# Both feed-forward sublayers as seven products of quarters, on one NeuronCore

## The reference, cut

```python
def swiglu(x, w_gu, w_down):
    a, u = jnp.split(x @ w_gu, 2, axis=-1)      # 1024 -> 2 x 2816
    return (jax.nn.silu(a) * u) @ w_down        # 2816 -> 1024

def ffn_sublayer(x, w_gu, w_down, g, b):
    return layer_norm(ALPHA * x + 0.5 * swiglu(x, w_gu, w_down), g, b)
```

## Time and profile before

| | us |
|---|---|
| runs (3): median, lowest, highest | 1947.2, 1946.07, 1953.2 |
| profiled execution: span from first to last instruction | 1943.7 |
| first feed-forward stretch | 27.86 to 427 |
| second feed-forward stretch | 1519.4 to 1921 |

### The profile page before, as it was taken

How to read it: one execution, slowest core, us unless ns; L and a number is a source line. 1 busy time by engine, 2 the same in 40 slices (tenths; PEclk the granted TensorE clock), 3 DMA queues, 4 the chain that set the end, 5 groups by cost and what they waited for, 6 DMA issues and landing times.

```text
span 1943.7 us, 33105 instructions
## 1 busy us (share of the span) xinstructions
PE 1804.9 (93%) x13247; PEld 1699.9 (87%) x13247; DVE 778.9 (40%) x1081; ACT 667.4 (34%) x899; POOL 85.2 (4%) x113
## 2 busy tenths in 40 slices
PE   6999999998997768999989999999999899999996
PEld 5999999987997537878768999869998799999996
DVE  2333332234223875756663223344345433333123
ACT  3333331124223555666563222124322433332111
POOL 0000000000002420000000000110000000000002
PEclk9999999999997998999989999999999999999998
DMA  4222222230440015767752232062223022222221
GB/s 142 91 90 91 89 84 82 81 108 22 133 133 23 1 51 176 273 228 249 242 169 91 87 98 84 17 215 66 91 91 100 22 86 87 89 90 84 92 97 46
DMA packets 146659, 203.75 MB, mean 105 GB/s; under 512 B 5538, under 2 KB 127330, under 8 KB 146594
## 3 DMA queue, kind: packets, MB, share of 16 engines
q1 hardware_dynamic: 145442, 198.35, 31.4%
q0 software_dynamic: 1152, 4.46, 0.6%
HBM read 191.39 MB, written 11.40 MB: 104 GB/s over the span
## 4 chain that ended last, share of the span: by engine, by line
PE 88%; DVE 4%; ACT 4%; issue 2%; DMA 0%; SPq 0%; POOL 0%; ACTq 0%; POOLq 0%; DVEq 0%
PE ps L297 68%; PE ps L1201 4%; PE ps L1232 3%; PE ps L1187 2%; PE ps L974 1%; PE ps L988 1%; PE ps L614 1%; PE ps L1624 1%; PE ps L1211 1%; PE ps L1616 1%; PE ps L1248 1%; PE ps L699 1%; PE ps L1198 1%; ACT aT L1069 1%; PE ps L981 0%
## 5 line engine op out<-in xcount | busy, mean ns | idle before, releaser
L297 PE MATMUL ps<-xh,w_hi_t 128*128 128x272 f32 x2432 | 510.1, 291 | 25.3 <-DVE xl L651 18.3
L297 PE MATMUL ps<-xh,w_lo_t 128*128 128x272 f32 x2432 | 505.9, 290 | 0.0
L297 PE MATMUL ps<-xl,w_hi_t 128*128 128x272 f32 x2432 | 504.2, 289 | 0.0
L283 DVE TENSOR_TENSOR w_lo_t<-w_raw,w_hi_t 128x2048 fp32r<-128x2048 f32 (+1 forms) x112 | 252.4, 2254 | 519.2 <-ACT w_hi_t L279 519.2
L297 PEld LDWEIGHTS ps<-xh,w_hi_t 128*128 128x128 f32 x2432 | 385.0, 190 | 30.2 <-issue 20.7
L297 PEld LDWEIGHTS ps<-xl,w_hi_t 128*128 128x128 f32 x2432 | 385.1, 190 | 0.0
L297 PEld LDWEIGHTS ps<-xh,w_lo_t 128*128 128x128 f32 x2432 | 382.4, 190 | 0.0
L279 ACT CAST w_hi_t<-w_raw 128x2048 fp32r<-128x2048 f32 (+1 forms) x112 | 209.9, 1874 | 276.5 <-PE ps L297 276.5
L297 PE MATMUL ps<-hh,w_lo_t 128*128 128x272 f32 x704 | 145.7, 288 | 0.0
L297 PE MATMUL ps<-hh,w_hi_t 128*128 128x272 f32 x704 | 145.5, 288 | 0.0
L297 PE MATMUL ps<-hl,w_hi_t 128*128 128x272 f32 x704 | 145.1, 288 | 0.0
(11 more groups left out here) (245 smaller groups left out, 2107.0 us busy)
## 6 DMA issues: line engine op xcount, KB each, us to landing
w_raw<-in_ffn_w_gu_dram SPq DMA_DIRECT2D x44, 1024.0 KB, 5.1
w_raw<-in_w_in_dram SPq DMA_DIRECT2D x32, 1024.0 KB, 5.7
k_page<-in_cache_k_dram SPq DMA_DIRECT2D x64, 512.0 KB, 4.8
v_page<-in_cache_v_dram SPq DMA_DIRECT2D x64, 512.0 KB, 4.6
w_raw<-in_ffn_w_down_dram SPq DMA_DIRECT2D x16, 1024.0 KB, 5.1
w_raw<-in_ffn_w_down_dram SPq DMA_DIRECT2D x8, 768.0 KB, 4.7
w_raw<-in_w_branch_a_dram SPq DMA_DIRECT2D x4, 1024.0 KB, 5.2
st_in<-in_state_ret_dram SPq DMA_DIRECT2D x8, 512.0 KB, 5.0
```

The lines of the kernel that those rows point to most:

```text
L283: nc.vector.tensor_tensor(w_lo_t[:, j, 0:nk], w_raw[:, j, 0:nk], w_hi_t[:, j, 0:nk].bitcast(F32), ALU.subtract).then_inc(lo_split, 1)
L297: mm = nc.tensor.matmul(ps[:, bank + half, 0:HALF], w[:, j, k, w_cols], m[:, k0 + k, half * HALF:half * HALF + HALF], start=start and k == ...
```

## The change

Each unit of work is one block of 256 output columns, seen as 2 x 2 quarters: weights by k parity and by which 128 columns, x by k parity and by token half. Seven products of quarters (Winograd's form of Strassen) replace the eight. Four products need sums of weight quarters (`f_sum`, made by POOL in `weight_sum`), x is held in seven forms (`xc_hi`, `xc_lo`; four of them sums made by POOL in `pool_x`), the hidden values likewise (`hc_hi`, `hc_lo`, four pairs at a time; POOL in `pool_drain`). The results are put together from PSUM copies (ACT), PSUM additions (DVE) and, for the down units, additions into `xT` on POOL. Six slots of split weight quarters and three raw chunks are held. The down projection is taken in four parts of the depth (hidden pairs 0 to 1, 2 to 4, 5 to 7, 8 to 10), each as four units behind the pairs that it needs. A unit's products stand in a row: P1, P5, P6, P2, P7, P3, P4, with P1, P6, P7 and P4 in one PSUM bank, P5 and P3 in another, P2 in a third. The feed-forward code has no hardware loops. `ln1` splits the first chunks of the k projection itself, `ln2` makes no split x, the transposition at the start makes plain x only, the out projection splits no chunk for the stage behind it. Buffers move, some semaphores are shared.

The diff, cut to its core:

```diff
+A_OF = {"P1": (0, 0), "P2": (1, 0), "P4": (1, 1)}
+B_OF = {"P1": 0, "P2": 1, "P5": 2, "P6": 3, "P7": 4, "P4": 5, "P3": 6}
+SUM_OF = {"P5": "1", "P6": "2", "P7": "3", "P3": "4"}
...
+def ffn_plan():
+    units, pairs = [], 0
+    for lo, hi in ((0, 2), (2, 5), (5, 8), (8, KF // 2)):
+        while pairs < min(hi + 1, KF // 2):
+            units += [("g", pairs, 0, KP), ("u", pairs, 0, KP)]
+            pairs += 1
+        units += [("d", m, lo, hi) for m in range(4)]
+    def whole(n, q):
+        return n, q, *units[n][2:]
+    entries = [whole(n, q) for n in range(len(units)) for q in ("P1", "P5", "P6", "P2", "P7", "P3", "P4")]
+    return units, entries
...
+            def pe_part(self, pe):
+                for e, (n, q, k0, k1) in enumerate(self.entries):
+                    s = self.slot_of[n, q]
+                    pe.wait_ge(self.w_lo, self.s0 + s + 1)
+                    kind, _, lo, _ = self.units[n]
+                    if kind == "d":
+                        pe.wait_ge(self.h_lo, KF // 2 * self.i + k1)
+                    elif n < 2:
+                        pe.wait_ge(self.x_lo, 7 * self.i + B_OF[q] + 1)
+                    first = k0 == lo
+                    if q == "P1":
+                        if first and n >= 3:
+                            self.c21_read(pe, n - 3)
+                        dst = self.x_bank(n)
+                    elif q == "P2":
+                        if first and n >= 2:
+                            pe.wait_ge(self.c11, self.n0 + n - 1)
+                        dst = self.z_bank(n)
+                    elif q == "P5":
+                        if first and n >= 2:
+                            pe.wait_ge(self.c12, self.n0 + n - 1)
+                        dst = self.y_bank(n)
+                    elif q == "P6":
+                        pe.wait_ge(self.u1_kept, self.n0 + n + 1)
+                        dst = self.x_bank(n)
+                    elif q == "P7":
+                        pe.wait_ge(self.u2_kept, self.n0 + n + 1)
+                        dst = self.x_bank(n)
+                    elif q == "P4":
+                        pe.wait_ge(self.c22, self.n0 + n + 1)
+                        dst = self.x_bank(n)
+                    else:
+                        pe.wait_ge(self.p5_kept, self.n0 + n + 1)
+                        dst = self.y_bank(n)
+                    opens = q in ("P1", "P2", "P5") and first
+                    for k in range(k0, k1):
+                        if kind == "d":
+                            b_hi, b_lo = hc_hi[:, k % PAIRS, B_OF[q]], hc_lo[:, k % PAIRS, B_OF[q]]
+                        else:
+                            b_hi, b_lo = xc_hi[:, B_OF[q], k], xc_lo[:, B_OF[q], k]
+                        a_hi, a_lo = f_hi[:, s % SLOTS, k - lo], f_lo[:, s % SLOTS, k - lo]
+                        for t, (wt, m) in enumerate(((a_hi, b_hi), (a_hi, b_lo), (a_lo, b_hi))):
+                            mm = nc.tensor.matmul(dst, wt, m, start=opens and k == k0 and t == 0,
+                                                  stop=k == k1 - 1 and t == 2, skip_group_check=True)
+                    mm.then_inc(self.product, 1)
...
+            def split_hi(self, act, s):
+                n, q = self.slots[s]
+                if q in SUM_OF:
+                    self.summed(act, n, SUM_OF[q])
+                else:
+                    self.raw_ready(act, n)
+                if s >= SLOTS:
+                    self.made(act, *self.slots[s - SLOTS])
...
+            def weight_sum(self, pool, n, q):
+                self.raw_ready(pool, n)
+                if n:
+                    pool.wait_ge(self.w_lo, self.s0 + self.slot_of[n - 1, P_OF[q]] + 1)
+                out = f_sum[:, int(q) - 1, 0:self.depth(n)]
+                if q == "1":
+                    if n:
+                        self.summed(pool, n - 1, "2")
+                    nc.gpsimd.tensor_tensor(out, self.raw(n, 0, 1), self.raw(n, 1, 1), ALU.add).then_inc(self.w_sum, 1)
...
+            def pool_x(self, pool):
+                t1, t2, t3, t4 = (xc_raw[:, j] for j in (2, 3, 4, 5))
+                c = 4 * self.i
+                self.x_ready(pool)
+                nc.gpsimd.tensor_tensor(t1, self.quarter(0, 1), self.quarter(0, 0), ALU.subtract).then_inc(self.x_sum4, 1)
+                pool.wait_ge(self.x_sum4, c + 1)
+                nc.gpsimd.tensor_tensor(t2, self.quarter(1, 1), t1, ALU.subtract).then_inc(self.x_sum4, 1)
+                pool.wait_ge(self.x_sum4, c + 2)
+                nc.gpsimd.tensor_tensor(t4, self.quarter(1, 0), t2, ALU.subtract).then_inc(self.x_sum4, 1)
+                nc.gpsimd.tensor_tensor(t3, self.quarter(1, 1), self.quarter(0, 1), ALU.subtract).then_inc(self.x_sum4, 1)
...
+            def dve_x(self, dve):
+                for j in range(7):
+                    dve.wait_ge(self.x_hi, 7 * self.i + j + 1)
+                    if j in (2, 3):
+                        dve.wait_ge(self.x_sum4, 4 * self.i + j)
+                    nc.vector.tensor_tensor(xc_lo[:, j], self.b_operand(j), xc_hi[:, j].bitcast(F32), ALU.subtract
+                                            ).then_inc(self.x_lo, 1)
...
+                elif q == "P7":
+                    self.made(dve, n, q)
+                    dve.wait_ge(self.p5_kept, self.n0 + n + 1)
+                    nc.vector.tensor_tensor(self.out(n, "22"), self.out(n, "22"), self.x_bank(n), ALU.add
+                                            ).then_inc(self.c22, 1)
...
+            def dve_part(self, dve):
+                for s in range(SLOTS):
+                    self.split_lo(dve, s)
+                self.dve_x(dve)
+                for e in range(len(self.entries)):
+                    self.dve_drain(dve, e)
+                    for p in range(KF // 2):
+                        if e == self.hidden_entry(p, 5):
+                            self.dve_hidden(dve, p)
+                    for m in range(3):
+                        if e == self.done[self.unit_of["d", m, KF // 2], "P4"] + 2:
+                            self.dve_norm(dve, m)
+                    for s in self.split_at[e]:
+                        self.split_lo(dve, s)
+                self.dve_norm(dve, 3)
...
+                elif q == "P3":
+                    pool.wait_ge(self.c12, self.n0 + n + 1)
+                    if kind == "u":
+                        c, t = 4 * (KF // 2 * self.i + i), hc_raw[:, i % PAIRS]
+                        nc.gpsimd.tensor_tensor(b12[:], b12[:], gate[:, i % 2, 2], ALU.mult).then_inc(self.h_mul, 1)
+                        pool.wait_ge(self.h_mul, 3 * (KF // 2 * self.i + i + 1))
+                        nc.gpsimd.tensor_tensor(t[:, 2], b12[:], t[:, 0], ALU.subtract).then_inc(self.h_sum, 1)
+                        nc.gpsimd.tensor_tensor(t[:, 4], t[:, 6], b12[:], ALU.subtract).then_inc(self.h_sum, 1)
+                        pool.wait_ge(self.h_sum, c + 1)
+                        nc.gpsimd.tensor_tensor(t[:, 3], t[:, 6], t[:, 2], ALU.subtract).then_inc(self.h_sum, 1)
+                        pool.wait_ge(self.h_sum, c + 3)
+                        self.c21_read(pool, n)
+                        nc.gpsimd.tensor_tensor(t[:, 5], t[:, 1], t[:, 3], ALU.subtract).then_inc(self.h_sum, 1)
...
+            def pool_part(self, pool):
+                for q in "1234":
+                    self.weight_sum(pool, 0, q)
+                for s in range(SLOTS):
+                    self.pool_after(pool, s)
+                self.pool_x(pool)
+                for e in range(len(self.entries)):
+                    self.pool_drain(pool, e)
+                    for s in self.split_at[e]:
+                        self.pool_after(pool, s)
+            def pool_after(self, pool, s):
+                n, q = self.slots[s]
+                if q in SUM_OF and n + 1 < self.N:
+                    self.weight_sum(pool, n + 1, SUM_OF[q])
...
+                if self.split:
+                    split_hi(act, 0, 0, 0)
+                    split_hi(act, 1, 0, 1)
                 for k in range(KD):
                     act.wait_ge(self.scaled, KD * self.i + k + 1)
-                    nc.scalar.activation(xh[:, k], xT[:, k], ACT.Identity, bias=self.bias(k)).then_inc(self.y_hi, 1)
+                    if self.split:
...
+                if self.split:
+                    split_lo(dve, 0, 0)
+                    split_lo(dve, 1, 1)
                 for k in range(KD):
-                    low(k)
```

More of the change, by code:

```diff
@@ L263, in build @@
         out_stored = sem("out_stored")
+        rows_landed = [sem(f"rows_landed{j}") for j in range(4)]
         def score_ps(row):
@@ new lines, in build @@
+            h_mul, h_sum, h_hi, h_lo = sem("f_h_mul"), sem("f_h_sum"), sem("f_h_hi"), sem("f_h_lo")
+            added = sem("f_added")
+            units, entries = ffn_plan()
+            N = len(units)
+            slot_of, done = {}, {}
+            for e, (n, q, _, _) in enumerate(entries):
+                slot_of.setdefault((n, q), len(slot_of))
+                done[n, q] = e + 1
```

(56 more changed lines are left out.)

546 lines of the change are left out of this document (321 added, 225 removed).

## The result

The change makes the kernel slower: median 2054.5 us of 4 runs against 1950.2 of 4 runs of the kernel before, a ratio of 1.0528 (95% interval 1.0502 to 1.0555). The forecast was 1975 with a range to 2035: the direction was right, the size was off by 80 us.

A forecast was written before the change was run, and what follows sets the result against it. The prediction took PE as the bound before the change and the SBUF port shared by DVE and POOL after it. Starts +40 and twice -6 gave +28 on 1947.2: 1975 us, range 1912 to 2035.

The forecast's parts named there:

- Matmuls: In each feed-forward sublayer, 3168 matmuls become 2772 at 0.125 us; 49.5 us less each if PE stays the bound.
- The starts: First units end later, +13.5 and +19 us; k projection's first splits, +4; low clock at both starts, +3: +40.
- The sum from the first unit's end: From the first unit's end to the sublayer's end: 379 us instead of 385, 6 less in each sublayer.
- the third rival: Products in a row: P4 waits for DVE's addition, 68 us on top of PE's 1903, giving 1971; chance 0.18.
- the port: In the feed-forward, DVE and POOL exclude each other on SBUF columns; this sets the pace, 22.1 to 25.0 us per pair.
- PE's 1903: Rival: PE stays the feed-forward bound, 42 us less per sublayer, 1903; chance 0.27 together with the port's low end.
- The pair's 23.5 us: Port time per gate and up pair, taken near a sampled sequence between 22.1 and 25.0 us; PE needs 21.0.
- The down units' 8.4 and 6.4 us: Port time per down unit of depth 3 and 2, against PE's 7.9 and 5.25 us.
- The low clock: PE stands longer between its first products at both sublayer starts and runs at a lower clock: +3 us.
- the whole-duration exclusion: Rival: DVE and POOL exclude each other for whole instructions in the feed-forward; 27.3 us per pair, 2111; chance 0.06.
- The signs that it named: Feed-forward profile: PE some 85% busy, longer splits and weight sums, ACT waiting for POOL, a pair every 23 to 24 us.
- the sign for the third rival: If P4's wait on DVE's addition leads and ACT never waits for POOL, the third rival holds.

The follow-up runs named there:

- The table of four versions: Whole or short weight sums, each with products in a row or P4 later: 2054.5 and 1992.7 us whole, 1959.2 and 1919.3 short.
- P4 later: The change with P4 placed behind P1 and P5 of the next unit, except ahead of the last group: 1992.7 us, ratio 1.0210.
- the run with the hidden cast later: The change with ACT's cast and DVE's low part of a pair's hidden values three products later: 2019.5 us, ratio 1.0347.
- the last two runs on the chain: Eight-product down units, gate and up products in a row: 1936.3 us; the same with POOL's hidden-quarter sums and wider cast and low part restored: 1985.6 us.
- short sums: The change with POOL's four weight sums per unit covering only the first pair of k tiles: 1959.2 us, ratio 1.0037.
- short additions: The change with POOL's three additions to x per down unit covering one column instead of 272: 2041.3 us, ratio 1.0453.
- plain down units: The change with P4 later and the down projection as eight products, without POOL's weight sums, hidden-quarter sums or additions there: 1927.1 us, ratio 0.9870.
- the start reordered: Plain down units, with POOL's x sums ahead of unit 1's weight sums and x taken between the first weights: 1917.0 us, ratio 0.9817.

## Why the prediction was right in direction and wrong in size

**Matmuls:** right, 2772 each, 0.126 us.

**The starts:** right. The first unit ends at 56.1 (55 forecast); in the second sublayer ACT's first cast is at 1580.85, the sums of x end 22.0 us after it (21.6) and the unit ends 34.7 after it (33). All four terms of the starts were +40; in the profiled executions, where the span grew by 110, what the stretches from the first units' ends leave is 47. The excess lies mostly between the two sublayers.

**The sum from the first unit's end:** wrong, 417.0 and 415.7 us where it said 379. Term by term in the first sublayer (each unit from its first product to that of the next):

| term | forecast | measured |
|---|---|---|
| gate and up units | 248 | 254.2 |
| four down units of depth 2 | 26 | 34.7 |
| twelve of depth 3 | 101 | 119.6 |
| wait for the last pair | 4.5 | 8.5 |

Twice 38 is 75 of the 80 us.

**The step that failed** is the sentence against the third rival: "where the port sets the pace these waits lie within it". It made the port and the handoff alternatives, and put the waits ahead of P4 at nothing in the sum; they were 50.2 us in the first sublayer. The table of four versions shows that the two costs add: the weight sums cost 73 with P4 later, and the forecast had priced the port at 72 (1975 less PE's 1903); the order then cost 62 more, where the rival had 68. With P4 later, the case that the forecast describes, the time is 1992.7, within 18 of its 1975. That the rival's 68 is so near 62 is in part luck: it had a wait in every gate and up unit and 38 us in the down units, and measured were 100 us over both sublayers, none of them in the up units and 56 in the down units, of which the later P4 gives back only a part. (The prediction calls its rivals' times spans; they are worked out from the median of 1947.2 and compare with 1975 as they stand.)

**The pair's 23.5 us** came out nearly right (254.2 for 248) by luck, for another reason than the one given. With P4 later the same sums and splits fit into some 234 us, 22.2 a pair, near the lower end of 22.1. What fills the change's 254 is P4's 21.4 and the low clock behind it. (The sample that gave 23.5 is read a little short: the first of its four operations was issued at 612.78, ahead of 613.12, so part of its fixed time lies outside the 1.29 us.) The forecast had "ACT ... covered" by its busy time of 14.5 us per pair; but the queue is in order, and a cast that waits for POOL holds the casts behind it, as at 206.33 above. That this wait is at work the run with the hidden cast later and the last two runs on the chain show.

**The down units' 8.4 and 6.4 us** were too low even as a port price: with P4 later they still take 9.5 and 8.05, where PE waits for ACT's copies and these for POOL's additions, a chain that the forecast had not. With short sums in a row they are at 8.7 and 7.2. For each us of POOL's busy time taken away, the short weight sums gave 0.48 us (95 of 199) and the short additions 0.18 (13 of 73, not told from nothing), so the sum of columns is not the right measure with the products in a row. That what counts is which DVE operation a POOL sum delays is a reading of the timelines, not shown by a run of its own. How much is work of the last pair that runs over into the down units was not separated.

**The low clock:** +3 forecast, for the two starts alone; 20 us in each sublayer measured, as PE stands over 0.5 us 28 times in the first and 25 in the second. With plain down units it stands twice in each, and 3 us are lost.

**The rivals.** PE as the bound fell for the change, though 1919 with short sums and P4 later comes within 16 of its 1903. By the whole-duration exclusion the stretch from the first unit's end would be 447 us; it was 417 in the change and 389 with P4 later. The rule of the Trainium skill ("SBUF — State Buffer", section "SBUF: two separate sides") that the lock is held for the whole instruction is thus not borne out here either, if the whole recorded duration is meant. The chance of 0.58 for slower was on the right side; the range's upper end of 2035 was 20 too low because the forecast's high end and the third rival were never added. The signs that it named came true almost to the number (PE 85% busy, splits of 1.01, sums of 1.31 to 1.58, a pair every 24.2 us, ACT waiting for POOL's sums), but the port with the handoff gives them as well as the port alone; and as P4's wait leads while ACT does wait for POOL, the sign for the third rival decided nothing.

## What to carry to other kernels

Two costs that the trace supports are alternatives only if one hides the other; a rate (a shared port) and a latency (an in-order queue ahead of a bank that is used again at once) added up here, and PE's longer standstills cost low-clock time on top (20 us beside 74.5 of standing). An engine at 43% is no cover where one of its instructions waits for a slower engine: read what is queued behind the waiting instruction. Fewer multiplications seem to pay where a unit has enough matmuls for the sums that they need: with seven products in gate and up (84 matmuls a unit) and eight in the down projection (63 or 42 with seven) the kernel was 1.3% faster than before, or 1.8% with the start reordered, and with seven in both and P4 later 2.1% slower. That the matmuls per unit make the difference was not tested apart from the hidden sums and the additions that went along.

## What was not expected of the hardware

After 2.9 us without matmuls PE restarted at a granted clock of 0.52 (211.54 to 214.00), while after the shorter stop ahead of 254.57 (0.71 us) it stayed at 1.00 and its matmuls followed 0.13 us apart from the second on. And the price of POOL's work was not the same everywhere: a us of weight sums taken away gave 0.48 us, a us of additions to x 0.18, if anything.
